# First norm of a hybrid encoder layer: squares, scaling and turns beside the modulation products, scale and shift by channel block

## The chip, the cores and the metric

The kernel runs on one core of a Trainium2 chip. The metric is the device time of one execution in microseconds (us). The engines are TensorE (PE, its weight loads PEld), VectorE (DVE), ScalarE (ACT), GpSimd (POOL) and SyncE (SP); each runs its own list of instructions in order, and they meet at semaphores. SP, ACT and POOL also issue transfers.

## The reference, cut to what matters

One step of an encoder layer over 1024 prompt rows and 8 x 16 sample rows, D = 1024, all float32. The part around the change:

```python
mod = (jax.nn.silu(c) @ w_ada[l] + b_ada[l])[:, None, :]
sh_m, sc_m, g_m, sh_f, sc_f, g_f = jnp.split(mod, 6, axis=-1)
h = rmsnorm(x, norm_mix_w[l]) * (1.0 + sc_m) + sh_m
...
z, xbc, dt, q, k, v = jnp.split(h @ w_in, SPLITS, axis=-1)
xbc, new_conv = causal_dwconv(xbc, conv_hist, conv_w, conv_b)
```

`c` has nine rows (one for the prompt, one for each sample). After this follow a scan over chunks, attention, an output projection, and a second norm with a gated feed-forward network.

## The kernel before

**Numbers in two parts.** The large products are computed as three products of numbers rounded to fp32r: every operand is split into a high part (a rounding copy) and a low part (the operand less its high part). A weight unit is 128 columns of a weight matrix (128x1024 elements). SP loads it into one of three buffers of `weights_raw`, ACT makes `weights_hi` (`w_hi(n)`), POOL makes `weights_lo` (`w_lo(n)`), and PE multiplies. SP loads unit n when the low part of unit n-3 is made; `w_hi(n)` waits for the products of unit n-3.

**Setup and modulation ("ada" phase, 0 to 44 us).** SP issues 20 small loads (`setup_in`), then four pieces of `w_ada` of 2 MB into three buffers `WA`. PE waits for all 20, turns the rows of `c` (after a SiLU on ACT) and the small vectors, and multiplies the turned condition `cond_T` with the pieces: per piece eight products of 128x32 by 128x512, a copy of the result into `mod_rows` on DVE (semaphore `ada_row`), and a sum over partition groups on PE (`ada_sum`), to which DVE adds the bias (`ada_out`). Pieces 0, 1 give the shift `SCOL[:, 0]`, pieces 2, 3 the scale `AM`, both as columns by channel. All engines meet at `phase_end`.

**First norm (44 to 106 us).** `norm_tiles` goes over nine tiles of 128 rows. ACT issues the load of a tile into one of two buffers `x_rows`, takes the squares with their sum (L1726) and the root (L1727); DVE takes the reciprocal (L1126) and scales the rows (L1127); PE turns the tile by eight transposes of 128x128 (L514) into two banks; DVE applies scale and shift from the banks, one instruction for each channel block of 128 (L1104; for the sample tile two, L1116 and L1117) into `h_raw`; ACT copies it to `h_hi` (L1720) and POOL makes `h_lo` (L2132). Both have shape [128, 8 channel blocks, 1152 rows].

**Input projection (from 106 us).** `in_unit(n)` multiplies unit n with three groups of 384 rows, 24 instructions to a group (L571 to L573), into banks 0 to 2 in turn. Units 0 to 7 are the channels of the convolution: ACT copies each group from its bank (`proj_out`, L1770 and L1774), DVE convolves a unit (L1175 to L1181) once its three groups are out, and ACT applies a SiLU (`xbc_silu`). Groups 0 and 1 of unit 0 stand between the turns of the first norm, and so do four of the `late_pair`s: a late pair multiplies two more pieces of 0.5 MB of `w_ada` (32 pieces in all, for the other four sections of the modulation), and `late_sum` sums a section. The rest of them stand in `late_slot(n)`, behind unit n. SP's queue holds, in order, the four pieces, units 0 to 2, pairs 0 and 1, and so on; a pair's pieces wait for the products of an earlier pair.

The order on PE after the phase's end:

```python
for j in range(NT):
    turn_tile(0, j, HNORM, BANKS_1)
    if j in (5, 8):
        in_unit(0, [j // 3 - 1])
    if j in PAIRS_AT_NORM:
        late_pair(PAIRS_AT_NORM.index(j))
in_unit(0, [2])
late_slot(0)
for n in range(1, 9):
    in_unit(n)
    if n < 7:
        late_slot(n)
```

Of the kernel before, what the change touches and what calls it, by code (L numbers as in the profile page):

```python
# [78 lines left out]
def build(nc, a, o):  # L79
# [93 lines left out]
    HL = r("h_lo", [P, KT, T], F32R)  # L173
    XBC = at("xbc_T", [P, 8, T], R2)
    ZT = at("z_T", [P, 4, T], R3)
    r = Region(R2 + 4 * T * 4, R3)
    HNORM = r("x_normed", [P, 2, D])
    HRAW = r("h_raw", [P, 2, KT, P])
# [11 lines left out]
    CT = r("cond_T", [P, KT, 32])  # L190
    TAILR = at("ssm_tail_rows", [27, D], xr_off)
# [114 lines left out]
    with ctx:  # L306
# [17 lines left out]
        def mark(ins, name):  # L324
# [6 lines left out]
            "pe_once": ["dt_raw", "dt_turned", "tails_turned", "sums", "state_turned", "yo_rows", "bias_turned", "ffn_turned"],  # L331
# [46 lines left out]

        def unit_used(n):

            if n < N_OUT0:
                return sem("proj"), 3 * (n + 1)
# [54 lines left out]
        N_SETUP = 20  # L437
        OUT_NORM_AT = [4, 6]
        BANKS_1, BANKS_2 = [4, 6] * 5, [6, 6, 6, 4, 6, 4]
# [13 lines left out]
        PAIRS_AT_NORM = [2, 4, 6, 8]  # L453
# [3 lines left out]
        def _(sp):  # L457
# [22 lines left out]
            for c in range(4):  # L480
                if c >= 3:
                    sp.wait_ge(sem("ada_used"), c - 2)
                sp.dma_start(WA[c % 3][:, :, :], a["w_ada"][0, :, c * 512:(c + 1) * 512]
                             .rearrange("(k p) n -> p k n", p=P)).then_inc(sem(f"ada_in{c % 3}"), 16)
# [25 lines left out]
        def _(pe):  # L510
# [5 lines left out]
            pe.wait_ge(sem("setup_in"), 16 * N_SETUP)  # L516
            pe.wait_ge(*once("cond_silu"))
            for k in range(KT):
                turn(PS[:, 0, k * NCOND:(k + 1) * NCOND], CROWS[:, k * P:(k + 1) * P], NCOND)
            turn(PS[:, 0, 80:101], VROW[:, :], 21)  # L520
            turn(PS[:, 0, 104:152], BROW[:, :], 48).then_inc(sem("setup_turned"), 1)
            for k in range(KT):
                mm = turn(PS[:, 1, k * 29:(k + 1) * 29], SROW[:, k * P:(k + 1) * P], 29)
            mm.then_inc(sem("setup_turned"), 1)
            pe.matmul(PS[0:NH, 2, 0:384], RELB[:, :], ONEHOT[:, :], start=True, stop=True)\
              .then_inc(sem("setup_turned"), 1)

# [11 lines left out]
            pe.wait_ge(*once("cond_T"))  # L539
            for c in range(4):  # L540
# [8 lines left out]
                if c >= 1:  # L549
# [39 lines left out]
            def late_sum(s):  # L589
                pe.wait_ge(sem("ada_row"), 4 + s + 1)  # L590
                if s == 0:
                    pe.wait_ge(sem("h_raw"), 2 * NT)
                else:
                    pe.wait_ge(sem("ada_sum_out"), 4 + s)
# [16 lines left out]
            def in_unit(n, groups=range(NG)):  # L611
                weights_ready(pe, n)
                for g in groups:
                    if n == 0:
                        pe.wait_ge(sem("h_lo"), 3 * (g + 1))
                    q = 3 * n + g
                    if q >= 3:
                        pe.wait_ge(sem("proj_out"), q - 2)
                    mm = products(PS[:, q % 3, 0:TG],
                                  [(WH[n % 3][:, k * P:(k + 1) * P], WL[n % 3][:, k * P:(k + 1) * P],  # L620
                                    HH[:, k, g * TG:(g + 1) * TG], HL[:, k, g * TG:(g + 1) * TG]) for k in range(KT)])
                    mm.then_inc(sem("proj"), 1)


            for j in range(NT):
                turn_tile(0, j, HNORM, BANKS_1)
                if j in (5, 8):
                    in_unit(0, [j // 3 - 1])
                if j in PAIRS_AT_NORM:
                    late_pair(PAIRS_AT_NORM.index(j))  # L630
            in_unit(0, [2])
            late_slot(0)
            for n in range(1, 9):
                in_unit(n)
                if n < 7:
                    late_slot(n)
# [295 lines left out]
            for g in range(3):  # L932
                for f in range(KT):
# [27 lines left out]
                    if g == 2 and f in OUT_NORM_AT:  # L961
                        turn_tile(NT, OUT_NORM_AT.index(f), N2, BANKS_2)

            turn_tile(NT, 2, N2, BANKS_2)
            pe.wait_ge(sem("mix_out"), 18)
            for j in range(3, 5):
                turn_tile(NT, j, N2, BANKS_2)
# [8 lines left out]
            for i, (u, g) in enumerate(UP_ORDER):  # L976
                weights_ready(pe, N_FFN0 + u)
                if i in (0, 3):
                    pe.wait_ge(sem("h_lo"), NT + 3 * (g + 1))
# [3 lines left out]
                if i < 1:  # L983
                    turn_tile(NT, 6 - 1 + i, N2, BANKS_2)

            def turn_late(jj):
                pe.wait_ge(sem("normed"), NT + 6 + jj + 1)
                if jj == 0:
                    pe.wait_ge(sem("up_out"), NUP0)
                else:  # L990
                    pe.wait_ge(sem("h_raw"), 2 * (NT + 6 + jj))
# [6 lines left out]
            for s, (kind, grp, i) in enumerate(MIXED):  # L998
                n = N_MIXED + s
                weights_ready(pe, n)  # L1000
                if kind == "u":
                    if i == 0:
                        pe.wait_ge(sem("h_lo"), NT + NT)
# [39 lines left out]
        def _(ve):  # L1043
# [7 lines left out]

            ve.wait_ge(sem("setup_in"), 16 * N_SETUP)
            ch(ve.tensor_tensor(LQK[:, 0, :], LQK[:, 0, :], LQK[:, 1, :], ALU.mult))
            ch(ve.tensor_tensor(LQK[:, 2, :], LQK[:, 2, :], LQK[:, 3, :], ALU.mult))
# [1251 lines left out]
```

## Time and profile before

| | |
|---|---|
| median of 3 runs | 1859.39 us (1858.83 to 1861.01) |
| the profiled execution | 1859.56 us, its span 1857.8 us |
| mean granted TensorE clock | 0.946 of full speed |
| PE busy | 1651.0 us (89%) |
| DVE busy | 986.8 us (53%) |
| ACT busy | 628.7 us (34%) |
| POOL busy | 443.2 us (24%) |
| read from HBM, written | 173.62 MB, 17.11 MB |

The span is counted from the first to the last instruction. An engine's busy time counts its instructions alone; in a row of the profile the time in square brackets is the idle time just before it, with what ended it. "Granted clock" is the share of full speed (2.4 GHz) that TensorE was given. Where PE is busy throughout, its work sets the time; where it is not, the question is which engine or transfer it waits for.

### The profile page before, as it was taken

How to read it: one execution, taken by the hardware profiler on the slowest of the kernel's cores; microseconds unless marked ns; L12 is line 12 of the kernel's file. 1: busy time of each engine (PE TensorE's matmuls, PEld its weight loads, DVE VectorE, ACT ScalarE, POOL GpSimd, SP SyncE). 2: the span in 40 equal slices, each digit the busy share in tenths (PEclk: the TensorE clock that was granted, in tenths of full speed). 3: DMA queues.
4: the chain of work that ended last, by engine and by line, in shares of the span. 5: the costliest groups of instructions: out<-in, count | busy, mean ns of one | idle time of the engine just before them, and what ended most of it. 6: DMA issues, size and time to landing. Idle time of an engine off the chain costs nothing. (4 is left out here: it accounts for less than half of the span.)

```text
span 1857.8 us, 23796 instructions
## 1 busy us (share of the span) xinstructions
PE 1651.0 (89%) x9399; PEld 1461.4 (79%) x9399; DVE 986.8 (53%) x1686; ACT 628.7 (34%) x1137; POOL 443.2 (24%) x270
## 2 busy tenths in 40 slices
PE   4489998779998987758968999999999999999896
PEld 1378987659996665637758999999978988999775
DVE  1665515860003665453345666666546677667744
ACT  1422222302112663342242222322444444444532
POOL 0331111113220000026554333323261111111132
PEclk9689999979998998978988999999999999999998
DMA  8545110112123002605561222122245434444442
GB/s 284 191 151 170 35 35 3 45 45 67 48 83 131 1 1 69 227 12 146 192 227 45 64 64 68 57 68 81 68 128 167 132 107 147 134 150 125 145 155 72
DMA packets 164564, 192.27 MB, mean 103 GB/s; under 512 B 7858, under 2 KB 126875, under 8 KB 164416
## 3 DMA queue, kind: packets, MB, share of 16 engines
q1 hardware_dynamic: 139626, 132.11, 23.1%
q10 hardware_dynamic: 19612, 40.93, 6.8%
q0 software_dynamic: 5216, 17.71, 2.7%
q8 instruction: 75, 1.23, 0.3%
q14 instruction: 35, 0.29, 0.0%
HBM read 173.62 MB, written 17.11 MB: 103 GB/s over the span
## 5 line engine op out<-in xcount | busy, mean ns | idle before, releaser
L571 PE MATMUL PS<-h_hi,weights_hi 128*128 128x384 f32 x1280 | 436.6, 341 | 11.0 <-POOL h_lo L2132 6.4
L572 PE MATMUL PS<-h_lo,weights_hi 128*128 128x384 f32 x1280 | 433.9, 339 | 0.0
L573 PE MATMUL PS<-h_hi,weights_lo 128*128 128x384 f32 x1280 | 433.6, 339 | 0.0
L2119 POOL TENSOR_TENSOR weights_lo<-weights_raw,weights_hi 128x1024 fp32r<-128x1024 f32 x99 | 252.7, 2554 | 754.2 <-ACT weights_hi L1697 731.9
L1697 ACT ACTIVATE weights_hi<-weights_raw 128x1024 fp32r<-128x1024 f32 x202 | 213.7, 1058 | 217.8 <-PE PS L1022 105.0
L571 PEld LDWEIGHTS PS<-h_hi,weights_hi 128*128 128x128 f32 x1280 | 244.1, 191 | 17.9 <-issue 13.2
L572 PEld LDWEIGHTS PS<-h_lo,weights_hi 128*128 128x128 f32 x1280 | 244.0, 191 | 0.0
L573 PEld LDWEIGHTS PS<-h_hi,weights_lo 128*128 128x128 f32 x1280 | 243.7, 190 | 0.0
L1020 PE MATMUL PS<-weights_hi,g_hi 128*128 128x512 f32 x396 | 160.9, 406 | 15.2 <-DVE weights_lo L1644 12.9
L2247 POOL TENSOR_TENSOR g_lo<-g_T,g_hi 128x384 fp32r<-128x384 f32 x66 | 81.6, 1237 | 372.3 <-ACT g_hi L2014 372.3
L1021 PE MATMUL PS<-weights_lo,g_hi 128*128 128x512 f32 x396 | 158.9, 401 | 0.0
L1022 PE MATMUL PS<-weights_hi,g_lo 128*128 128x512 f32 x396 | 158.3, 400 | 0.0
L1644 DVE TENSOR_TENSOR weights_lo<-weights_raw,weights_hi 128x1024 fp32r<-128x1024 f32 x103 | 124.3, 1235 | 25.5 <-ACT weights_hi L1697 22.9
L572 PE MATMUL PS<-h_lo_b,weights_hi 128*128 128x384 f32 x352 | 118.5, 337 | 0.0
L571 PE MATMUL PS<-h_hi_b,weights_hi 128*128 128x384 f32 x352 | 118.4, 336 | 0.0
L573 PE MATMUL PS<-h_hi_b,weights_lo 128*128 128x384 f32 x352 | 118.4, 336 | 0.0
L1020 PEld LDWEIGHTS PS<-weights_hi,g_hi 128*128 128x128 f32 x396 | 75.6, 191 | 34.2 <-DVE weights_lo L1644 15.0
L1022 PEld LDWEIGHTS PS<-weights_hi,g_lo 128*128 128x128 f32 x396 | 75.7, 191 | 18.2
L1021 PEld LDWEIGHTS PS<-weights_lo,g_hi 128*128 128x128 f32 x396 | 76.1, 192 | 15.6
L1554 DVE SCALAR_TENSOR_TENSOR val<-up_val,ffn_conv_cols,val 128x768 f32<-128x768 f32 x44 | 83.7, 1903 | 1.6
L1554 DVE SCALAR_TENSOR_TENSOR gate<-up_gate,ffn_conv_cols,gate 128x768 f32<-128x768 f32 x44 | 83.3, 1894 | 1.5
L2032 ACT ACTIVATE up_val<-PS 128x384 f32<-128x384 f32 x44 | 21.6, 491 | 141.4 <-PE PS L573 141.4
(365 smaller groups left out, 2526.8 us busy)
## 6 DMA issues: line engine op xcount, KB each, us to landing
weights_raw<-in_w_up_dram SPq DMA_DIRECT2D x88, 512.0 KB, 3.9
weights_raw<-in_w_down_dram SPq DMA_DIRECT2D x66, 512.0 KB, 4.5
w_ada_unit<-in_w_ada_dram SPq DMA_DIRECT2D x32, 512.0 KB, 5.6
weights_raw<-in_w_in_dram SPq DMA_DIRECT2D x24, 512.0 KB, 4.1
weights_raw<-in_w_out_dram SPq DMA_DIRECT2D x24, 512.0 KB, 4.1
w_ada<-in_w_ada_dram SPq DMA_DIRECT2D x4, 2048.0 KB, 16.1
k_cache<-in_cache_k_dram ACTq DMA_DIRECT2D x8, 1024.0 KB, 5.6
x_scratch<-x_new POOLq DMA_DIRECT2D x9, 512.0 KB, 6.2
```

What stands on the lines that cost most here:

```text
L571: pe.matmul(out, wh, xh, start=(i == 0), stop=False)
L572: pe.matmul(out, wh, xl, start=False, stop=False)
L573: mm = pe.matmul(out, wl, xh, start=False, stop=(i == n - 1))
L1020: pe.matmul(out, GH[i % 2][:, lhs], WH[n % 3][:, ws], start=(f == 0), stop=False)
L1021: pe.matmul(out, GH[i % 2][:, lhs], WL[n % 3][:, ws], start=False, stop=False)
L1022: mm = pe.matmul(out, GL[i % 2][:, lhs], WH[n % 3][:, ws], start=False, stop=(f == FT - 1))
L1554: ins = ve.scalar_tensor_tensor(out=d, in0=src, scalar=w, in1=d, op0=ALU.mult, op1=ALU.add)
L1644: mark(ve.tensor_tensor(WL[n % 3][:, :], WR[:, n % 3, :], WH[n % 3][:, :].bitcast(F32), ALU.subtract), "w_lo_dve")
L1697: mark(ac.activation(WH[n % 3][:, :], WR[:, n % 3, :], ACT.Copy), "w_hi")
L2032: mark(ac.activation(U[:, 2 + g * TG:2 + (g + 1) * TG], PS[:, i % 8, 0:TG], ACT.Copy), "up_out")
L2119: mark(gp.tensor_tensor(WL[n % 3][:, :], WR[:, n % 3, :], WH[n % 3][:, :].bitcast(F32), ALU.subtract), "w_lo")
L2247: mark(gp.tensor_tensor(GL[i % 2][:, :], GT[:, f, gg * TG:(gg + 1) * TG], GH[i % 2][:, :].bitcast(F32), ALU.subtract), "g_lo")
```

## The change

- The nine tiles of x are loaded at the very start from ACT's queue into a buffer of their own, `XIN` (it lies where `xbc_T` lies later). SP's queue begins with the two loads of `c`, the constants (together a semaphore `cond_in`) and pieces 0 and 1 of `w_ada`; then come the other 17 small loads (`setup_in`), then pieces 2 and 3.
- In the ada phase, the tiles go in three groups of three. ACT takes squares and roots; DVE scales three tiles in place (`x_norm`); PE turns them (`x_turn`), four channel blocks to bank 2 and four to bank 3; DVE copies the first half back into `XIN` (`x_out`), ACT the second. A group stands ahead of each of the products with pieces 0, 1 and 2. The turns of the small vectors and their copies stand behind the products with piece 0.
- `w_lo(0)` and `w_lo(1)` on POOL stand ahead of the end of the phase.
- After the phase, for each group of 384 rows and each channel block, ACT writes `h_hi` from `XIN` with scale and shift in one instruction (128x384, `mod_hi`), and DVE makes `h_lo` in two: x times scale less `h_hi`, then plus shift (`mod_lo`). In the last group the blocks have 256 prompt rows, and the sample rows go by themselves in four wide instructions. POOL makes no `h_lo` here.
- PE does late pairs 0 and 1, then group 0 of units 0 and 1, pair 2, group 1 of both, pair 3, group 2 of both, and then each late slot ahead of a unit from unit 2 on. ACT copies the groups out in that order, and the SiLU of unit 0's convolution stands directly behind the sixth copy.
- `norm_tiles` of the second norm counts its semaphores from 0; nothing else there changes.

```diff
+XIN = at("x_T", [P, NT, KT, P], R2)
-HNORM = r("x_normed", [P, 2, D])
-HRAW = r("h_raw", [P, 2, KT, P])
+XSQ = at("x_squares_unread", [P, 3, D], R4)
...
 # SP
-setup(CONST[:, :], const_dram[:, :])
-setup(CROW[0:1, :], a["c_prompt"])
-setup(CROW[1:NCOND, :], a["c_sample"])
+sp.dma_start(CROW[0:1, :], a["c_prompt"]).then_inc(sem("cond_in"), 16)
+sp.dma_start(CROW[1:NCOND, :], a["c_sample"]).then_inc(sem("cond_in"), 16)
+sp.dma_start(CONST[:, :], const_dram[:, :]).then_inc(sem("cond_in"), 16)
+ada_in(0)
+ada_in(1)
 setup(VROW[0:8, :], ...)
...
-for c in range(4):
-    if c >= 3:
-        sp.wait_ge(sem("ada_used"), c - 2)
-    sp.dma_start(WA[c % 3][:, :, :], ...)
+ada_in(2)
+ada_in(3)
...
 # PE
+def x_turn(j):
+    pe.wait_ge(sem("x_normed"), j + 1)
+    for half in range(2):
+        if j >= 1:
+            pe.wait_ge(sem("xT_act" if half else "xT_dve"), j)
+        for k in range(4 * half, 4 * half + 4):
+            mm = turn(PS[:, 2 + half, k % 4 * P:(k % 4 + 1) * P], XIN[:, j, k, :])
+        mm.then_inc(sem("x_turned"), 1)
...
 for c in range(4):
+    if c < 3:
+        for j in range(3 * c, 3 * c + 3):
+            x_turn(j)
+    ada_products(c)
+    if c == 0:
+        setup_turns()
+    else:
+        ada_sum(c - 1)
 ada_sum(3)
...
+late_pair(0)
+late_pair(1)
+for g in range(NG):
+    in_group(0, g)
+    in_group(1, g)
+    if g < 2:
+        late_pair(2 + g)
+for n in range(2, 9):
+    late_slot(n - 2)
     in_unit(n)
...
 # DVE
 for c in range(4):
+    if c < 3:
+        x_norm(c)
+        for j in range(3 * c, 3 * c + 3):
+            x_out(j)
     ve.wait_ge(sem("ada_used"), c + 1)
...
+def modulate(g):
...
+    for k in range(KT):
+        x = XIN[:, 3 * g:3 * g + n, k, :]
+        ve.wait_ge(sem("mod_hi"), KT * g + k + 1)
+        ch(ve.scalar_tensor_tensor(out=x, in0=x, scalar=AM[:, k, 0:1],
+                                   in1=HH[:, k, cols].bitcast(F32).rearrange("p (j n) -> p j n", j=n),
+                                   op0=ALU.mult, op1=ALU.subtract))
+        mark(ve.tensor_scalar(HL[:, k, cols].rearrange("p (j n) -> p j n", j=n), x,
+                              SCOL[:, 0, k, 0:1], None, ALU.add), "mod_lo")
...
 # ACT
+for j in range(NT):
+    load(XIN[:, j, :, :], x_all[j].rearrange("p (k n) -> p k n", k=KT), f"x_in{j // 3}")
+ac.wait_ge(sem("cond_in"), 48)
 out(ac.activation(CROWS[:, :], CROW[:, :], ACT.Silu), "act_once")
+for g in range(3):
+    ac.wait_ge(sem(f"x_in{g}"), 48)
+    for j in range(3 * g, 3 * g + 3):
+        mark(ac.activation(XSQ[:, j % 3, :]..., XIN[:, j, :, :], ACT.Square, accum_out=STAT[:, 48 + j:49 + j]), "act_step")
+    again(ac, "act_step")
+    mark(ac.activation(STAT[:, 3 * g:3 * g + 3], STAT[:, 48 + 3 * g:51 + 3 * g], ACT.Sqrt, ...), "x_sd")
+    for j in range(3 * g, 3 * g + 3):
+        ac.wait_ge(sem("x_turned"), 2 * j + 2)
+        mark(ac.activation(XIN[:, j, 4:8, :], PS[:, 3, :]..., ACT.Copy), "xT_act")
 w_hi(0)
 w_hi(1)
...
+        mark(ac.activation(HH[:, k, cols]..., XIN[:, 3 * g:3 * g + n, k, :],
+                           ACT.Identity, scale=AM[:, k, 0:1], bias=SCOL[:, 0, k, 0:1]), "mod_hi")
```

## Rows read from the trace of the kernel before

**Rows 1.** The page's chain that ended last, shares by engine.

```profile
PE 40%; DVE 4%; POOL 1%; ACT 1%; issue 1%; DMA 0%; DVEq 0%; ACTq 0%
```

**Rows 2.** Windows: stretch, length, busy us (count) of PE, PEld, DVE, ACT, POOL, clock, DMA, GB/s.

```profile
14.00:38.00 24.00, 15.23 (x84) 6.08 (x84) 5.27 (x16) 0.97 (x1) 0.66 (x1) 1.00 1.05 387
...
44.20:106.50 62.30, 30.16 (x152) 22.32 (x152) 38.65 (x99) 25.57 (x40) 26.03 (x12) 0.67 0.52 174
106.50:128.60 22.10, 22.01 (x116) 18.93 (x116) 10.96 (x17) 2.48 (x5) 5.19 (x3) 0.92 0.45 145
128.60:263.00 134.40, 134.40 (x811) 118.64 (x811) 64.26 (x99) 35.62 (x57) 22.67 (x10) 1.00 0.30 97
```

**Rows 3.** Timeline of the ada phase: start us, length us, engine, instruction.

```profile
8.75 15.43 SPq L483 DMA_DIRECT2D w_ada<-in_w_ada_dram  x4
...
13.92 1.05 ACT L1700 ACTIVATE cond_silu<-cond_rows 9x1024 f32<-9x1024 f32 x1 [11.90 <-DMA lambda_vectors<-in_lambda_k_dram]
...
18.97 0.18 DVE L1058 COPY vector_cols<-PS 128x21 f32<-128x21 f32 x1 [4.05 <-PE PS L525]
...
27.19 3.64 PE L546 MATMUL PS<-w_ada,cond_T 128*32 128x512 f32 x16 [3.44 <-DMA w_ada<-in_w_ada_dram]
...
32.60 1.93 PE L546 MATMUL PS<-w_ada,cond_T 128*32 128x512 f32 x16 [0.47 <-DMA w_ada<-in_w_ada_dram]
...
34.45 1.06 PE L535 MATMUL PS<-CONST,mod_rows 128*128 128x9 f32 x8
34.64 0.69 DVE L1078 COPY mod_rows<-PS 128x512 f32<-128x512 f32 x1 [2.21 <-PE PS L546]
...
43.85 0.23 DVE L1084 SCALAR_TENSOR_TENSOR scale_mix_cols<-mod_cols,vector_cols 128x72 f32<-128x72 f32 x1
```

**Rows 4.** The line of the four loads of `w_ada` pieces, L483: issue to landing.

```profile
DMA to landing us min/median/max: 10.4/16.1/22.7
```

**Rows 5.** Waits from 44.2 to 106.5 us: total us, times, longest.

```profile
ACT x_normed L1726 <- DMA x_rows<-in_x_prompt_dram: 20.0, 6, 5.3
```

**Rows 6.** Timeline of the first norm, one tile's instructions and a later turn.

```profile
58.75 1.06 ACT L1726 ACTIVATE x_normed<-x_rows 128x1024 f32<-128x1024 f32 x1 [2.07 <-DMA x_rows<-in_x_prompt_dram]
...
60.82 0.75 DVE L1127 TENSOR_SCALAR x_normed<-x_rows,stats 128x1024 f32<-128x1024 f32 x1 [0.30 <-DVE stats L1126]
...
61.63 1.97 PE L514 MATMUL PS<-CONST,x_normed 128*128 128x128 f32 x8 [1.44 <-DVE x_normed L1127]
...
73.81 1.09 PE L514 MATMUL PS<-CONST,x_normed 128*128 128x128 f32 x8 [1.33 <-DVE x_normed L1127]
```

**Rows 7.** Timeline of PE where it becomes busy throughout.

```profile
106.59 0.66 PE L571 MATMUL PS<-h_hi,weights_hi 128*128 128x384 f32 x1 [5.74 <-POOL h_lo L2132]
...
112.47 1.46 PE L597 MATMUL PS<-mod_rows_late,CONST 128*9 128x512 f32 x3
...
116.00 0.45 PE L571 MATMUL PS<-h_hi,weights_hi 128*128 128x384 f32 x1
...
128.69 1.92 PE L584 MATMUL PS<-w_ada_unit,cond_T 128*32 128x512 f32 x16
```

**Rows 8.** Timeline of DVE, POOL and ACT in the first convolution.

```profile
113.24 0.75 DVE L1175 TENSOR_SCALAR conv_acc<-conv_in,ssm_conv_cols 128x1024 f32<-128x1024 f32 x1 [3.95 <-ACT conv_in L1774]
113.91 0.28 DVE L1176 TENSOR_SCALAR conv_acc<-conv_in,ssm_conv_cols 128x128 f32<-128x128 f32 x1
...
114.15 2.37 POOL L2119 TENSOR_TENSOR weights_lo<-weights_raw,weights_hi 128x1024 fp32r<-128x1024 f32 x1 [5.39 <-ACT weights_hi L1697]
114.22 3.38 DVE L1178 SCALAR_TENSOR_TENSOR conv_acc<-conv_in,ssm_conv_cols,conv_acc 128x1024 f32<-128x1024 f32 x1
...
117.90 1.28 DVE L1178 SCALAR_TENSOR_TENSOR conv_acc<-conv_in,ssm_conv_cols,conv_acc 128x1024 f32<-128x1024 f32 x1
119.10 0.35 DVE L1181 SCALAR_TENSOR_TENSOR conv_acc<-conv_in,ssm_conv_cols,conv_acc 128x128 f32<-128x128 f32 x1
...
120.48 0.49 ACT L1770 ACTIVATE conv_in<-PS 128x384 f32<-128x384 f32 x1 [6.40 <-PE PS L573]
```

More of the change, by code:

```diff
@@ L537, in ada_sum, with ada_products @@
                 mm.then_inc(sem("ada_summed"), 1)
-            pe.wait_ge(*once("cond_T"))
-            for c in range(4):
+            def ada_products(c):
                 pe.wait_ge(sem(f"ada_in{c % 3}"), 16 * (c // 3 + 1))
@@ L548, in _ @@
                 mm.then_inc(sem("ada_used"), 1)
-                if c >= 1:
+            pe.wait_ge(*once("cond_T"))
+            for c in range(4):
+                if c < 3:
[5 more added lines that the diff above has]
+                else:
                     ada_sum(c - 1)
@@ L1059, in _, with x_norm @@
[L1059 removed]
             ch(ve.memset(CT[:, :, :], 0.0))
+            ve.wait_ge(*once("cond_turned"))
             out(ve.tensor_copy(CT[:, :, 0:NCOND], PS[:, 0, 0:72].rearrange("p (k c) -> p k c", k=KT)), "dve_once")
[L1062 to L1064 removed]
+            def x_norm(g):
+                ve.wait_ge(sem("x_sd"), g + 1)
+                ch(ve.reciprocal(STAT[:, 16 + 3 * g:19 + 3 * g], STAT[:, 3 * g:3 * g + 3]))
+                for j in range(3 * g, 3 * g + 3):
+                    mark(ve.tensor_scalar(XIN[:, j, :, :], XIN[:, j, :, :], STAT[:, 16 + j:17 + j], None, ALU.mult), "x_normed")
@@ L1080, in _ @@
                     ada_out(c - 1)
+                else:
+                    setup_cols()
             ada_out(3)
@@ L1751, in _, with in_rows_out, xbc_silu @@
             load(WDT[:, :, :], a["w_in"][0, :, 1536:1544].rearrange("(k p) n -> p k n", p=P), "wdt_in")
-            for n in range(12):
+            def in_rows_out(n, g):
+                q = IN_ORDER.index((n, g))
+                ac.wait_ge(sem("proj"), q + 1)
+                src = PS[:, q % 3, 0:TG]
+                if n >= 8:
+                    mark(ac.activation(ZT[:, n - 8, g * TG:(g + 1) * TG], src, ACT.Silu), "proj_out")
+                    return
+                R = XRAW[:, n % 2, :]
+                c1 = min(TG, SEQ - g * TG)
+                ins = ac.activation(R[:, 3 + g * TG:3 + g * TG + c1], src[:, 0:c1], ACT.Copy)
+                if c1 < TG:
+                    mark(ins, "act_step")
+                    smp = R[:, 3 + SEQ:XB_W].rearrange("p (b t) -> p b t", b=NB)
+                    ins = ac.activation(smp[:, :, 3:3 + TS], src[:, c1:TG].rearrange("p (b t) -> p b t", b=NB), ACT.Copy)
+                mark(ins, "proj_out")
+            def xbc_silu(c):
+                ac.wait_ge(sem("conv"), c + 1)
+                mark(ac.activation(XBC[:, c, :], CACC[:, c % 2, :], ACT.Silu, bias=SSMC[:, c, 4:5]), "xbc_silu")
+            w_hi(2)
+            for q in range(6):
+                in_rows_out(*IN_ORDER[q])
+                if q == 4:
+                    w_hi(3)
+            xbc_silu(0)
+            for n in range(2, 12):
                 w_hi(n + 2)
@@ L2126, in _ @@
             gp.wait_ge(sem("bias_out"), 16)
+            w_lo(0)
+            w_lo(1)
             phase_end(gp, "ada")
@@ L2133, in norm_tile @@
                                       hi[:, :, c0:c0 + P].bitcast(F32), ALU.subtract), "h_lo")
-            w_lo(0)
-            w_lo(1)
-            for jj in range(NT):
-                norm_tile(0, jj, HRAW, HH, HL)
             for n in range(12):
```

201 lines of the change are left out of this document (103 added, 98 removed).

## The prediction, made before the changed kernel was run

> **What bounds the kernel now.** I read four views, in this order. The chain that ended last puts PE first by a wide margin [rows 1], so PE's idle stretches are where time can be won. The windows show where those are: from 106.5 us PE is busy 22.0 of 22.1 us and then 134.4 of 134.4 us, while from 44.2 to 106.5 us it is busy 30.2 of 62.3 us at a granted clock of 0.67 [rows 2]. The reader is to see there that in this stretch no engine is near full (DVE, the busiest, 38.7 of 62.3 us) and that the transfers are half used: it is a chain of single tiles. Third, the waits name its longest link: ACT waits six times, 20.0 us in all, for a tile of x, because two buffers let a load begin only when an earlier tile is done [rows 5]. Fourth, the timeline of the ada phase: the engines stand still until all 20 small loads are in (13.92 us), and from 14 to 38 us the transfers move 387 GB/s without a gap, PE waiting for each piece of `w_ada` [rows 2, 3]. So the ada phase is bound by transfers and the norm by a round trip, and the one could run beside the other.
>
> The measure of the change is when PE reaches unit 2 with nothing behind it. Before, unit 1 ends at 128.5 us, just before the pairs of late slot 1 (128.69) [rows 7]. In both orders the same work follows from there (late slot 1 and unit 2 only change places), and PE never waits up to 263 us [rows 2], so what is saved at this point stays saved unless something new stops PE later.
>
> **The change: transfers at the start.** Large transfers began to flow near 12 us (the first landed at 19.15, less its own 5.4 and a little of x, both worked out below); now almost nothing small stands before them, and I take 3 us. Data up to the last piece: 8.4 MB of `w_ada`, 4.7 MB of x, 0.64 MB of constants and 0.2 MB of small rows, 14 MB; at 0.387 MB/us [rows 2] 36 us, so the last piece lands near 40 us, against 38 before. How do the two queues share? Piece 0 was issued at 8.75 and landed 10.4 us later, at 19.15, with products on piece 1 from 27.19 and on piece 2 from 32.60 [rows 3, 4]. Piece 2 took 5.4 us alone, piece 1 8.0 us with two tiles of x (1.05 MB) beside it; the two tiles cost about 2.7 us of the common rate. I take half and half, 0.195 MB/us each. Then: constants near 6.3 us, the first three tiles near 11, piece 0 near 17, all of x near 27, piece 1 near 27.5, and the 17 small loads, which stand behind piece 1 in SP's queue, near 30 us. Bounds: 27 if they overtake, 33 if they are slow as at the start. Piece 3 is issued after the first products (about 26 us) while the queue is still full, and costs nothing.
>
> **The ada phase as a chain.** Squares of three tiles, root and reciprocal: 2.07 us for the last (58.75 to 60.82) and 2 x 1.2 before it, 4.5 us, and 0.75 for the scaling [rows 6]. First group from 11 us: PE can turn at about 17.5 (with 1.3 us allowed for ACT's first use of the root), three tiles by 1.97 us, 6 us, then products 3.64 us: near 26. The next link is the small loads, which hold PE's `setup_turns` and with them DVE's `setup_cols`, behind which `x_norm(1)` is queued. From 30.0:
>
> - the turns of the small vectors, about 3.1 us (from the SiLU's end at 14.97 to 18.97 PE turned condition and small vectors [rows 3]; I give the condition 0.9), and five copies of 1.8 us: 34.9;
> - reciprocal and one scaling: 35.9;
> - three tiles of turns: 1.97 us each at a low clock, 1.09 at the high one [rows 6], where the copy of half a bank (0.69 [rows 3]) keeps the period above 1.35. 4.0 to 5.9 us, taken 5.1: 41.0;
> - ACT can begin the third group's squares only behind its copies of the second: 0.6 + 3.9 + 0.3, 45.8. Products with piece 1 (1.93 to 3.64) and their sum (1.06 [rows 3]) run beside it;
> - reciprocal, scaling, turns, 0.95 + 4.8: 51.5;
> - products 2, sum, products 3, two sums with a copy of 0.69 between: 2.5 + 0.9 + 2.5 + 0.9 + 0.9: 59.2;
> - bias, `scale_cols` 0.23 [rows 3], meeting: 60.0.
>
> Products 1.93 at one end, 3.64 at the other, and the turns likewise, give 56 and 66 us for this point; it was 44.1 us. So the ada phase grows by 16 us. Which of PE's two levels holds is the largest unknown: the same 16 instructions took 3.64 us at 27.19 and 1.93 at 32.60, after PE had worked on [rows 3]; 1.93 is 2.4 GHz. I take values between, nearer the high level towards the end, since there PE has few gaps.
>
> **From there to the first product.** ACT writes a block of `h_hi` in about 0.5 us (0.49 for 128x384 out of a bank [rows 8]), DVE is slower and sets the pace. The scalar_tensor_tensor took 1.28 us at 1024 columns and 0.35 at 128, so 1.04 ns a column and 0.22 fixed: 0.62 at 384. The tensor_scalar took 0.75 at 1024 and 0.28 at 128 [rows 8], so 0.42 at 384, 0.34 to the next start. With the wait between, 0.98 us a block, 7.9 for eight; 9.4 if writing fp32r halves the second's rate, 7.0 if starts overlap more. First product at 60.0 + 0.6 + 7.9 = 68.5 us. Pairs 0 and 1 are on PE before it; their 2.1 MB, asked for at about 57, take 5.4 us and 2 of start, near 64.5, and are covered, by a microsecond or two at most.
>
> **From the first product on.** Three groups of unit 1 took from 116.00 to 128.5, 4.16 us each; the start at a low clock costs 1.65 more, as before (106.59 to 112.4 for the first [rows 7]). Six groups 24.9, low start 1.65, pairs 2 and 3 at 0.96 each, late slot 0 of 3.6 us (112.4 to 116.0 [rows 7]): unit 2 starts 32.1 us after the first product, at 100.6. Against 128.5 that is 27.9 us gained.
>
> Does DVE keep up? Group 1 is ready 7.9 us after group 0, and PE needs it after 10.9. Group 2 has eight blocks of 256 (0.79 us each) and three DVE instructions of 1.2 to 1.3 us on the sample rows: 10.1 us more, 18.0, against 20.2. Cover is 2.2 us. POOL's `w_lo(2)`, however, falls into group 2. In the convolution a DVE instruction that began beside `weights_lo` took 3.38 us where its like took 1.28 [rows 8]; 2.1 us, just covered. ACT's copies: the first group's copy stands behind all 25 instructions of `mod_hi`, three DMA issues and `w_hi(2)`, about 20.5 us after the meeting, and PE's fourth group needs it at about 21: nothing. `xbc_silu(0)` now stands directly behind the sixth copy and waits for a convolution of 8 to 10 us; queued behind it are `w_hi(4)` and unit 2's copies. It is ready about 37 us after the first product; PE fills its next three banks from 32 to 44.5, so that nothing waits. POOL loses nine `h_lo` of 2.4 us and DVE 64 small instructions: no gain, since neither was the bound.
>
> The Trainium skill, "SBUF — State Buffer", section "Who interferes with whom", says that a DVE instruction with two SBUF inputs, or one in a two-port mode, and a GpSimd instruction that reads SBUF exclude each other for the whole instruction. The trace agrees (3.38 against 1.28 us [rows 8]). By this rule the low parts of a group, once moved to DVE, are exposed to `w_lo(2)`, and `w_lo(0)`, `w_lo(1)` to DVE's scalings in the ada phase; it would add at most two of POOL's instructions, 4.7 us, an estimate that leaves the sign as it is.
>
> **Sum.** The profiled execution took 1859.56 us, 0.2 from the median of 1859.39, so the difference is taken from the median: 1859.4 - 27.9 = 1831.5 us. Own range of this case: the meeting at 56 to 66, blocks 7.0 to 9.4 for the group, a stall in group 2 of 0 to 4: gain 17 to 33, 1826 to 1842.
>
> **Rivals.**
> - *The slow ada phase.* PE stays at 1.2 GHz through all of it and the small loads land at 33 us: the meeting at 69, first product 77.5, gain 19, 1840 us. For: 0.67 in the norm stretch, where PE also worked in pieces [rows 2]. Against: PE has more work per gap now. The Trainium skill, "TensorE: Matmul & The Clock Gate", section "HAM oscillation — how this bites in real kernels", describes such a fall-back when work waits for data.
> - *DVE becomes the bound.* Blocks at 1.2 us and collisions with POOL in both later groups: first product 1.6 us later, stalls of about 6: gain 20, 1839 us. For: [rows 8]. Against: POOL has one instruction in the stretch.
> - *A quicker chain.* x and the small loads land early, turns at 1.09: meeting at 54, gain 34, 1825 us.
> - *Nothing gained.* PE is not held by the norm, and the later stages wait for a load or DVE at the same absolute time. Against: every later load waits for earlier products, and PE has no waits to 263 us. 1859 us.
> - *Slower.* The convolution becomes the bound of units 2 to 8. It starts with one unit more behind it, and each POOL instruction holds DVE for 2.1 us. DVE is busy 64 of 134 us there [rows 2]; a unit with its late slot takes PE 14.5 us. It decides from 18.5 us of DVE chain a unit, over seven units 28 us; at 19.5 it would be 35 - 27.9, 1866 us. The rows leave over 5 us of slack per unit.
>
> **Chances.** Forecast 0.55, slow ada phase 0.17, DVE the bound 0.10, quicker chain 0.11, nothing gained 0.03, slower 0.04. About 0.2% (3.7 us) is what a measurement of this kernel tells from no change. Faster 0.93, within 0.03, slower 0.04. The range 1822 to 1845 leaves out the last two, the far end of the quicker chain and mixtures of the two slow ones.
>
> **What the changed profile would show.** The small loads in near 30 us, with PE and DVE idle before; DVE's `scale_cols` at 56 to 66 us; blocks of `mod_lo` at about 1 us; the first L571-like product at 64 to 73 us; no PE wait over 1 us after it up to unit 2, which starts near 100; and later stages shifted by the same amount as that. Wrong would be: x taking more than its half of the rate and piece 0 late, blocks over 1.3 us, or PE waiting for `mod_lo` of groups 1 and 2.

## The result, and the profile after

The changed kernel took 1844.2 us (median of six executions, 1837.16 to 1850.38) against 1859.45 (1858.28 to 1863.74) of the kernel before: a ratio of 0.9914, 95% interval 0.9891 to 0.9937. It is faster, by 0.9%. The time lies in the range given last in the prediction (1822 to 1845), 0.8 us below its upper end, and above the range that it had added up from its own terms (1826 to 1842): 15.3 us were gained where 27.9 were forecast and 17 was the least. The profiled execution took 1844.83 us, its span is 1843.0 us, its mean granted clock 0.945 (0.946 before).

The chain that ended last is PE's still, by the page, and PE is busy for 90% of the span:

```profile
PE 41%; DVE 4%; POOL 1%; ACT 1%; issue 1%; DMA 0%; DVEq 0%; ACTq 0%
```

The windows of the changed kernel (columns as in [rows 2]):

```profile
14.00:38.00 24.00, 9.62 (x52) 5.88 (x52) 5.85 (x12) 5.77 (x12) 0.00 (x0) 0.77 0.94 331
0.00:14.00 14.00, 0.99 (x8) 0.92 (x8) 0.51 (x2) 6.57 (x9) 0.20 (x4) 1.00 0.88 329
...
106.00:244.00 138.00, 138.00 (x831) 119.39 (x829) 70.49 (x110) 35.70 (x57) 23.79 (x11) 1.00 0.35 114
43.90:65.00 21.10, 17.48 (x118) 11.44 (x116) 8.55 (x17) 8.28 (x14) 4.68 (x2) 0.84 0.26 68
```

From 14 to 38 us the transfers move 331 GB/s where they moved 387, and PE, which had 15.2 of 24 us of work there [rows 2], has 9.6. From 43.9 to 65 us it is busy 83% of the time. From 106 to 244 us it never stops, as in the same stretch of work before.

The timeline has the dates that the prediction names: first of PE and DVE in the ada phase, then of DVE and POOL in the modulation, then of PE again.

```profile
22.14 1.92 PE L568 MATMUL PS<-w_ada,cond_T 128*32 128x512 f32 x16 [1.10 <-DMA w_ada<-in_w_ada_dram]
...
35.50 0.29 PE L527 MATMUL PS<-CONST,vector_rows 21*128 21x21 f32 x1 [11.44 <-DMA lambda_vectors<-in_lambda_k_dram]
...
41.19 5.92 PE L527 MATMUL PS<-CONST,x_T 128*128 128x128 f32 x24 [2.79 <-DVE x_T L1088]
...
57.89 1.92 PE L568 MATMUL PS<-w_ada,cond_T 128*32 128x512 f32 x16
```

```profile
64.92 0.23 DVE L1131 SCALAR_TENSOR_TENSOR scale_mix_cols<-mod_cols,vector_cols 128x72 f32<-128x72 f32 x1
66.07 0.62 DVE L1210 SCALAR_TENSOR_TENSOR x_T<-x_T,scale_mix_cols,h_hi 128x384 f32<-128x384 f32 x1 [0.91 <-ACT h_hi L1830]
66.72 0.61 DVE L1213 TENSOR_SCALAR h_lo<-x_T,mod_cols 128x384 fp32r<-128x384 f32 x1
67.25 0.61 DVE L1210 SCALAR_TENSOR_TENSOR x_T<-x_T,scale_mix_cols,h_hi 128x384 f32<-128x384 f32 x1
...
89.45 0.35 DVE L1213 TENSOR_SCALAR h_lo<-x_T,mod_cols 128x256 fp32r<-128x256 f32 x1
...
90.23 2.38 DVE L1213 TENSOR_SCALAR h_lo<-x_T,mod_cols 128x256 fp32r<-128x256 f32 x1
```

```profile
89.98 2.48 POOL L2217 TENSOR_TENSOR weights_lo<-weights_raw,weights_hi 128x1024 fp32r<-128x1024 f32 x1 [25.61 <-ACT weights_hi L1766]
```

```profile
75.69 0.66 PE L602 MATMUL PS<-h_hi,weights_hi 128*128 128x384 f32 x1 [2.25 <-DVE h_lo L1213]
...
76.15 0.52 PE L603 MATMUL PS<-h_lo,weights_hi 128*128 128x384 f32 x1
...
81.54 0.34 PE L602 MATMUL PS<-h_hi,weights_hi 128*128 128x384 f32 x1
...
109.40 0.45 PE L602 MATMUL PS<-h_hi,weights_hi 128*128 128x384 f32 x1
```

The reader is to see four dates. All small loads are in at 35.5 us (forecast 30.0). `scale_cols`, DVE's row at 64.92 (`scale_mix_cols`), starts there (60.0 for it and the meeting behind it), 29.4 us later, where the chain was worked out at 30.0. The first product follows 10.77 us after it (8.5), at 75.69 (68.5). Unit 2 starts 33.7 us after that (32.1), at 109.40 (100.6). The whole of 8.8 us at unit 2 is in these rows: 5.5 - 0.6, 2.3 and 1.6.

In what follows, "the lead" is how much earlier than in the kernel before PE has the same number of instructions left. It is read where the kernel before stands at 290 us, and at the end. The changed kernel leads by 19.1 us at 290, by 18.2 at 700, by 14.2 at 960 and by 14.7 at the end. So 4.4 us more went in later stages, nearly all around the attention.

### The profile page after: what moved, and what is told of

It reads as the page before. It is cut to its first block and busy times, and to the rows that moved or that the text cites. A ratio compares the mean times of both kernels' runs of the same rounds, so it can differ in the third digit from the quotient of the medians.

```text
span 1843.0 us, 23788 instructions
## 1 busy us (share of the span) xinstructions
PE 1652.8 (90%) x9399; PEld 1464.0 (79%) x9399; DVE 990.8 (54%) x1660; ACT 636.7 (35%) x1156; POOL 424.3 (23%) x261
## 5 line engine op out<-in xcount | busy, mean ns | idle before, releaser
L602 PEld LDWEIGHTS PS<-h_hi,weights_hi 128*128 128x128 f32 x1280 | 243.7, 190 | 16.9 <-issue 12.2
L1048 PEld LDWEIGHTS PS<-weights_hi,g_hi 128*128 128x128 f32 x396 | 75.8, 191 | 34.2 <-DVE weights_lo L1713 14.7
```

The source lines that it names most:

```text
L602: pe.matmul(out, wh, xh, start=(i == 0), stop=False)
L1048: pe.matmul(out, GH[i % 2][:, lhs], WH[n % 3][:, ws], start=(f == 0), stop=False)
```

## Why the small loads come so late

SP's timeline shows an order that the forecast had not: the first of the 17 small loads blocks its queue for 13.31 us behind the two pieces, so that the others are issued from 18.27 to 25.06 us.

```profile
1.86 3.01 SPq L475 DMA_DIRECT2D w_ada<-in_w_ada_dram  x2
4.92 13.31 SPq L466 DMA_DIRECT2D vector_rows<-in_norm_mix_w_dram  x1
18.27 0.59 SPq L466 DMA_DIRECT2D vector_rows<-in_norm_ffn_w_dram  x1
...
25.11 7.00 SPq L475 DMA_DIRECT2D w_ada<-in_w_ada_dram  x2
```

The queues' packets in two stretches show how they shared and what the small loads are. From 13 to 19 us (q10 is ACT's queue with x, q1 SP's with `w_ada`):

```profile
DMA packets 845, 2.40 MB, mean 400 GB/s; under 512 B 48, under 2 KB 48, under 8 KB 845
...
q10 hardware_dynamic: 423, 1.54, 65.4%
q1 hardware_dynamic: 422, 0.86, 37.8%
```

and from 24 to 36 us:

```profile
DMA packets 2679, 3.22 MB, mean 268 GB/s; under 512 B 1148, under 2 KB 1249, under 8 KB 2679
```

The queues took turns by packets, 423 to 422. A packet of x holds 3.6 KB and one of `w_ada` 2.0 KB, so that x got 64% of the bytes, not half. Piece 0 came at 22.1 instead of 17. The Trainium skill, "DMA: Bandwidth & Descriptors", section "Queues, rings and completion order", says that each DMA engine goes round its queues packet by packet; the trace agrees (423 and 422). That x takes more than half and piece 0 comes late is the first of the prediction's own signs of being wrong. And 1148 packets of under 512 B, the small loads, pass in 12 us in which the transfers move 268 GB/s. The kernel before has them too, in its first 14 us, where its engines stand still:

```profile
DMA packets 1653, 1.51 MB, mean 108 GB/s; under 512 B 1151, under 2 KB 1252, under 8 KB 1653
```

The small loads are in 10.4 us after SP has issued the last of them (25.06). Whether the block at SP, the place behind piece 1, or these packets cost the 5.5 us was for the experiments to say.

## The experiments

Each ratio is to the kernel before in the same batch, with its 95% interval. The profiled marks are "`scale_cols` / first product / unit 2"; for the changed kernel they are 64.92 / 75.69 / 109.40.

### The small loads ahead of the pieces

```diff
+setup(VROW[0:8, :], ...)      # all 17
-ada_in(0)
-ada_in(1)
-setup(VROW[0:8, :], ...)      # all 17
+ada_in(0)
+ada_in(1)
```

> The 17 small loads stand ahead of the pieces of w_ada in SP's queue. Theory (SP's queue was blocked: the first small load took 13.3 us to issue behind the two big pieces, so the small loads landed at 35.5 us and held PE and DVE): they land near 13 us, scale_cols ends near 53 us instead of 65, the first product of unit 0 comes at about 63 instead of 75.7, and the time falls by 10 to 13 us against the changed kernel, to about 1832. Rival (the transfers set the ada phase: 14 MB at 0.387 MB/us): the pieces come later instead, PE waits for pieces 2 and 3, scale_cols stays above 61 us and the time falls by less than 4 us.

1841.6 us, ratio 0.9876 (0.9837 to 0.9914); 61.57 / 72.34 / 105.66. The wait for the small loads is gone, but piece 0 is now what PE waits for:

```profile
28.78 3.40 PE L568 MATMUL PS<-w_ada,cond_T 128*32 128x512 f32 x16 [6.75 <-DMA w_ada<-in_w_ada_dram]
```

The queues from 8 to 18 us:

```profile
DMA packets 1607, 3.28 MB, mean 328 GB/s; under 512 B 750, under 2 KB 837, under 8 KB 1607
...
q10 hardware_dynamic: 826, 3.01, 87.8%
q1 hardware_dynamic: 781, 0.27, 12.1%
```

In turn with x, SP's queue spent its 781 packets on 0.27 MB. My theory, 10 us or more from this order, fell. The rival came out in its numbers (`scale_cols` above 61 us, less than 4 us of time) and in its kind: a piece comes late instead. It is piece 0 that PE waits for, not pieces 2 and 3. The mark moved by 3.4 us.

### The small loads from POOL's queue

```diff
 # POOL, first in its list
+def gp_setup(dst, src):
+    store(dst, src, "setup_in")
+gp_setup(VROW[0:8, :], ...)   # all 17, taken out of SP's queue
```

> The 17 small loads are issued by POOL, SP issues the pieces of w_ada back to back. Theory (blocked queue): the small loads land by about 20 us, nothing stops SP between pieces 1 and 2, and the gain is that of the kernel with the small loads first or 1 us more, to about 1831. Rival (transfers set the phase): less than 4 us of gain. Second rival (POOL's issues are slow beside DVE): small loads at 30 us or later and half of the gain.

1842.3 us, ratio 0.9893 (0.9857 to 0.9929); 60.93 / 71.69 / 105.01. The theory (about 1831) fell, and the first rival (less than 4 us of gain) came out. SP issues the pieces from 1.86 us on with no small load among them, and PE waits for piece 0 until 28.43:

```profile
28.43 3.24 PE L552 MATMUL PS<-w_ada,cond_T 128*32 128x512 f32 x16 [6.82 <-DMA w_ada<-in_w_ada_dram]
```

The queues from 8 to 18 us, q0 being POOL's with the small loads:

```profile
q10 hardware_dynamic: 409, 1.47, 42.0%
q0 software_dynamic: 410, 0.28, 34.6%
q1 hardware_dynamic: 410, 0.84, 26.7%
```

Three queues take turns here, 409 to 410 to 410 packets, and SP's gets a third of them. So moving the small loads away from the block at SP is not enough: what they and x take from the transfers then lands on piece 0.

### The small loads between pieces 0 and 1

```diff
 ada_in(0)
-ada_in(1)
 setup(VROW[0:8, :], ...)      # all 17
+ada_in(1)
 ada_in(2)
```

> The 17 small loads stand behind piece 0 and ahead of piece 1 in SP's queue. Theory (two causes share the ada phase: with the small loads behind two pieces SP's queue was blocked to 18.3 us; with them ahead of all pieces piece 0 came at 28.8 us, because the loads of x take about two thirds of the transfers while they last): piece 0 lands near 22 us, the small loads near 24, nothing else waits for a transfer, scale_cols ends at 54 to 57 us against 64.9 of the changed kernel and 61.6 with the small loads first, and unit 2 starts 8 to 10 us earlier than in the changed kernel; the time is 1833 to 1838. Rival (the chain of turns and copies sets the phase whatever the loads do): scale_cols at 61 us or later, 1841.

1836.94 us, ratio 0.9885 (0.9863 to 0.9907); 59.61 / 70.38 / 103.69.

```profile
22.75 3.55 PE L568 MATMUL PS<-w_ada,cond_T 128*32 128x512 f32 x16 [1.59 <-DMA w_ada<-in_w_ada_dram]
...
29.48 0.23 PE L527 MATMUL PS<-CONST,vector_rows 21*128 21x21 f32 x1 [3.18 <-DMA lambda_vectors<-in_lambda_k_dram]
```

and its packets from 20 to 28 us:

```profile
DMA packets 1754, 1.56 MB, mean 195 GB/s; under 512 B 1049, under 2 KB 1150, under 8 KB 1754
```

Piece 0 keeps its date within 0.6 us. SP has issued the last small load at 19.27 us, 5.8 earlier, they are in 6.0 us earlier (10.2 after that issue) and `scale_cols` comes 5.3 us earlier: with the small loads where the forecast had put them (29.5 against 30.0), the mark falls where it had put it (59.6 against 60.0). The time (1833 to 1838) was hit, but `scale_cols` at 54 to 57 and unit 2 8 to 10 us earlier (it is 5.7) were too bright by what the small loads need, 29.5 instead of 24: 1049 small packets pass in the 8 us from 20 to 28, with the rate down to 195 GB/s. At 0.387 MB/us [rows 2] the 1.56 MB would have taken 4.0 us of these 8, and the 3.22 MB from 24 to 36 us in the changed kernel 8.3 of 12: by this estimate the small loads cost the transfers about 4 us in both places, and the stretches in which they pass are 8 and 12 us long. The run moves the small loads out from behind the block and ahead of piece 1 at once, so it doesn't tell these two apart; it does show that their date is what the mark follows.

### DVE's second instruction on one row of 384

In the changed kernel the second instruction reads x as three pieces of 128 (one per tile). Here the first writes to a contiguous scratch, and the second reads 384 columns.

```diff
-ch(ve.scalar_tensor_tensor(out=x, in0=x, ...))
-mark(ve.tensor_scalar(HL[:, k, cols].rearrange("p (j n) -> p j n", j=n), x, ...), "mod_lo")
+m = MTMP[:, k % 2, 0:n * P]
+ch(ve.scalar_tensor_tensor(out=m.rearrange("p (j n) -> p j n", j=n), in0=x, ...))
+mark(ve.tensor_scalar(HL[:, k, cols], m, ...), "mod_lo")
```

> DVE's first instruction of a block writes to a contiguous scratch row of 384, the second reads it from there, so that both sides of the second have one dimension of 384. Theory (the second took 0.61 us at 384 columns but 0.35 at 256 because its operands' outer dimensions, 3 and 384, keep it from the double rate, not because it writes fp32r): it takes 0.42 us, a block 0.98 instead of 1.17, the first product comes 1.5 us earlier, 1842 to 1843. Rival (384 columns into fp32r are slow in any shape): 0.61 us again and no change.

1844.25 us, ratio 0.9902 (0.9874 to 0.993); 64.58 / 73.82 / 106.62.

```profile
65.71 0.62 DVE L1212 SCALAR_TENSOR_TENSOR mod_tmp<-x_T,scale_mix_cols,h_hi 128x384 f32<-128x384 f32 x1 [0.90 <-ACT h_hi L1832]
66.36 0.42 DVE L1215 TENSOR_SCALAR h_lo<-mod_tmp,mod_cols 128x384 fp32r<-128x384 f32 x1
```

0.42 us instead of 0.61, for the same columns, written as fp32r in both: it is the shape of the operand, not fp32r writing, to which the prediction had put its bound of 9.4 us. The rows of the changed kernel say the same: 128x256, two pieces of 128, takes 0.35. The Trainium skill, "VectorE: DVE Perf Modes", section "What auto-detection actually checks", gives the double rate to a source and a destination whose outermost dimensions are both even, or equal. The trace agrees for two pieces (0.35) and for one row of 384 (0.42); three pieces against three, if the destination counts as such, would be equal and miss it all the same (0.61), which no run here goes into. The first product comes 9.24 us after `scale_cols` instead of 10.77. Unit 2 starts 32.8 us after the first product (33.7 in the changed kernel's first profile, 33.3 in its second). The lead at 290 us is 21.9, up from 19.1 (20.8 in a second execution of the changed kernel, below); the time of the whole (1842 to 1843 expected) doesn't show it, for a reason that the section on the spread comes to.

### Units 0 and 1 one after the other

```diff
 for g in range(NG):
     in_group(0, g)
-    in_group(1, g)
     if g < 2:
         late_pair(2 + g)
+in_unit(1)
```

> Units 0 and 1 no longer alternate: PE does the three groups of unit 0, then those of unit 1. Theory (DVE makes a group in 9.4 us, PE needs 4.2 for one unit): PE waits about 4 us for group 1 and again for group 2, unit 2 starts 7 to 8 us later, about 1852. Rival (the alternation is worth nothing, DVE is ahead anyway): 1844.

1852.48 us, ratio 0.9949 (0.9932 to 0.9966); 63.76 / 74.53 / 117.71. PE now waits for DVE, by the waits from 62 to 125 us (total, times, longest):

```profile
PE PS L602 <- DVE h_lo L1217: 6.5, 1, 6.5
...
PE PS L602 <- DVE h_lo L1213: 5.1, 2, 3.0
```

where the changed kernel has a single wait of this kind, before its first product:

```profile
PE PS L602 <- DVE h_lo L1213: 2.2, 1, 2.2
```

The theory came out, with waits of 3.0 and 6.5 us behind the first product where 4 and 4 were expected. The alternation is worth about 8 us of the gain (unit 2 is 9.5 us later relative to the first product). In the changed kernel's profile it just covers DVE's instruction of 2.38 us beside POOL's `weights_lo`; without it nothing covers that instruction.

### PE kept at work ahead of the first product

```diff
+for i in range(26):
+    turn(PS[:, 7, 0:P], C("ident"))
 late_pair(0)
 late_pair(1)
+for i in range(12):
+    turn(PS[:, 7, 0:P], C("ident"))
```

> PE does 26 idle turns of the identity into an unread bank ahead of pair 0 and 12 behind pair 1, otherwise the changed kernel. Theory (the first products run at 1.2 GHz to 81.3 us because PE was mostly idle from 64.7 to 75.7, and this costs 2.8 us): the clock is at 2.4 GHz from the first product on, the group takes 4.2 us instead of about 7, unit 2 starts 2 to 3 us earlier relative to the first product. The time falls by 2 us or less than the spread shows. Rival (the turns delay the pairs and the first product): first product later than 76.5, no gain or a loss of 1 us.

1846.77 us, ratio 0.9933 (0.991 to 0.9955); 66.08 / 76.84 / 110.15. The first products run at 0.34 us each from the start, 2.4 GHz, and group 0 of unit 0 takes 4.24 us instead of 6.88. But unit 2 still comes 33.3 us after the first product. What the products no longer take, PE now waits for. These are PE's waits on the way (the first is the one for group 0's low parts, as in every version):

```profile
76.84 0.41 PE L602 MATMUL PS<-h_hi,weights_hi 128*128 128x384 f32 x1 [1.01 <-DVE h_lo L1217]
...
91.45 0.42 PE L602 MATMUL PS<-h_hi,weights_hi 128*128 128x384 f32 x1 [0.68 <-ACT conv_in L1851]
...
98.12 0.41 PE L602 MATMUL PS<-h_hi,weights_hi 128*128 128x384 f32 x1 [1.27 <-issue]
```

The row at 98.12 is the start of group 2, 21.28 us after the first product. It names no releaser, but DVE's last low part of that group ends just before:

```profile
96.80 1.22 DVE L1221 TENSOR_TENSOR h_lo<-x_T,h_hi 128x1024 fp32r<-128x1024 f32 x1
```

Group 2 starts 21.28 or 21.29 us after the first product in four profiles without idle turns too (the changed kernel once more, and the small loads in each of their three other places), and unit 2 33.3 us after it in all five. Only the first profile of the changed kernel, whose group 0 was the slowest of these (6.88 us, against 5.80 to 6.38), has 21.65 and 33.7. So with these blocks DVE sets the date of group 2, and the expected 2 to 3 us weren't there. The rival's mark (first product later than 76.5, no gain) was met, but not by its cause: the first product follows `scale_cols` by 10.76 us as everywhere, and `scale_cols` itself, ahead of the idle turns, was 1.2 us late.

### All three, and without the idle turns

> The small loads behind piece 0, the contiguous scratch for DVE's second instruction, and the idle turns of PE, all three. Theory (the shortfall up to unit 2 is the sum of the three): scale_cols at 54 to 57 us, first product 9.2 us later at 64 to 66, unit 2 at 96 to 99 us against 109.4 of the changed kernel and 100.6 forecast; a time of 1829 to 1834. Rival (what is won at unit 2 is given back in the attention stage, whatever the clock does): lead of 30 us over the kernel before at unit 2, less than 18 at the end, 1841 or more in all runs.

The small loads between the pieces, the row of 384 and the idle turns: 1833.93 us, ratio 0.9867 (0.9849 to 0.9885); 58.82 / 68.06 / 99.86, lead 27.1 at 290 us, 25.8 at the end. The time was as expected (1829 to 1834) and the rival fell (25.8, not less than 18), but `scale_cols` and unit 2 were again 1 to 2 us later than expected. The forecast's own marks (60.0 / 68.5 / 100.6, 27.9) come out once its three wrong terms are put right.

> The small loads behind piece 0 and the contiguous scratch, without the idle turns of PE. Theory (from the run with the idle turns: with the clock already high PE only waits for DVE's low parts of group 2, so the turns bring nothing that lasts): unit 2 at 99 to 102 us as with the turns (100.3), time within 2 us of its 1833.9. Rival (the turns were worth their 2.8 us): unit 2 at 103, time 1836 to 1838.

Without the idle turns: 1838.95 us, ratio 0.9861 (0.9835 to 0.9888); 58.98 / 68.22 / 101.07, lead 27.4 at 290 us, 20.7 at the end. Unit 2 is where the theory had it (99 to 102), but the time is 5.0 us above that of the run with the turns, not within 2. The ratios, each to its own batch, hardly differ (0.9867 and 0.9861). From the first product to unit 2 it is 31.8 us with the turns and 32.85 without (32.8 with the row of 384 alone), so the turns are worth about 1.0 us when DVE is quick enough, from single profiles, and nothing that a ratio can tell.

### The third group's squares ahead of the second's copies

On top of the last version; ACT's order only.

```diff
+x_squares(0)
+x_copies(0)
+x_squares(1)
+x_squares(2)
+x_copies(1)
+x_copies(2)
```

> As the kernel with the small loads behind piece 0 and the scratch, and ACT takes the third group's squares ahead of its copies of the second group's turns, where it is idle. Theory (the squares of group 3 behind the copies end 0.9 us after DVE could scale, 51.28 against 50.37 us in the changed kernel): scale_cols comes 0.7 to 1.2 us earlier than without, unit 2 too, a time of 1832 to 1835. Rival (the scaling waits for the products with piece 1 and their sum as long): less than 0.4 us.

1835.5 us, ratio 0.9846 (0.9812 to 0.9881), the best ratio of all, though its interval overlaps that of the last version; 59.17 / 68.41 / 101.92. The reciprocal of the third group stands 1.1 us earlier, at 44.23:

```profile
44.23 0.18 DVE L1087 RECIPROCAL stats<-stats 128x3 f32<-128x3 f32 x1
```

but the products with piece 2, three rows of PE's timeline later, took part of their time at the low clock and gave it back:

```profile
51.09 2.97 PE L569 MATMUL PS<-w_ada,cond_T 128*32 128x512 f32 x16
```

(1.92 in the version without the edit). The expected 0.7 to 1.2 us at `scale_cols` was missed, and the time by 0.5 us; whether it is there at an equal clock stays open.

### The changed kernel once more: the spread

> The changed kernel once more, unchanged. Theory (the differences of several us between its own executions, and between its lead of 19 us at unit 2 and 14.7 at the end, are the granted clock's): its executions spread over 8 us or more again, the longer ones at a lower mean clock, about 1.9 us for each thousandth of the mean clock; the low stretches between 560 and 960 us are others than in the first profile, and so is the lead lost there. Rival (the lead is lost to a wait that the changed kernel has in the attention stage): the same 3 to 4 us lost in the same place, and PE idle for longer there.

1842.11 us, ratio 0.9906 (0.9886 to 0.9927); 63.61 / 74.37 / 107.68. The marks of one program thus differ by 1.3 to 1.7 us between two profiles. Three more versions are the same program up to `scale_cols` (64.58, 63.76 and 66.08), so that this mark spreads over 2.5 us in five profiles. By that measure the small loads first (61.57) or on POOL (60.93) are worth at least 2.0 us there, and between the pieces (58.8 to 59.6 in four profiles) at least 4.0. The distance from `scale_cols` to the first product is 10.76 or 10.77 us in every profile with the old blocks and 9.24 in every one with the row of 384. Its lead is 20.8 us at 290 and 20.7 at the end: nothing was lost in the attention. The windows of equal work there (in the kernel before, the first changed execution, and this one):

```profile
740.00:930.00 190.00, 151.08 (x1073) 116.95 (x1066) 78.23 (x156) 61.30 (x116) 66.31 (x39) 0.88 0.46 145
```

```profile
721.90:915.40 193.50, 154.55 (x1073) 119.13 (x1062) 78.23 (x156) 61.40 (x116) 66.39 (x39) 0.87 0.44 142
```

```profile
719.10:909.50 190.40, 149.13 (x1073) 115.40 (x1067) 78.27 (x156) 61.42 (x116) 66.39 (x39) 0.88 0.45 144
```

The same 1073 matmuls, DVE, ACT and POOL busy for the same time within 0.1 us; PE's busy time differs, 154.6 against 149.1 us, while its idle time goes the other way, 39.0 against 41.3. The first changed execution lost 3.5 us there and this one 0.4, with the same program. The other profiles sort the same way: between 290 us and the end, the seven with a mean granted clock of 0.940 to 0.947 gave back 3.4 to 9.8 us of their lead, three of the four with 0.949 to 0.951 gave back 0.1 to 1.3 us and the fourth gained 2.3. Over the twelve executions of the changed kernel the times go from 1837.16 to 1850.38 us and their mean granted clocks from 0.943 to 0.952, with a correlation of -0.95: about 1.5 us for a thousandth of clock (1.9 was expected). That the clock is the cause rests on this correlation and on PE's busy time at equal work; no run sets the clock.

## Why the prediction was right, and by how much it missed

- **What bounds, and that the norm can run beside the ada phase.** Right. PE reaches unit 2 at 109.4 instead of 128.5 us, with no stop behind it up to 244 us.
- **Transfers, "I take half and half, 0.195 MB/us each".** Wrong: the queues shared by packets, x got 64% of the bytes and piece 0 came at 22.1 instead of 17. PE lost nothing by that date in the changed kernel, where it stood idle for 11.4 us after these products, until the small loads were in. Whether the smaller share also kept SP's queue blocked for longer, and so the small loads late, no run separates.
- **"The 17 small loads ... near 30 us", bounds 27 to 33.** This is the term that failed most, 5.5 us: 35.5. It lies outside its own bounds. It counted their bytes (0.2 MB; the profile's list of issues adds up to 0.34) and not their 1148 packets, and it had no block at SP. With the small loads in at 29.5 us, in the run between pieces 0 and 1, the mark was 59.6. The kernel before had shown both the packets (1151 up to 14 us) and what they take (13.92 us, [rows 3]), and the prediction used that only for its upper bound of 33.
- **The chain from there, 30.0 us.** 29.4 to the start of `scale_cols`. The parts lie within about a microsecond of the forecast and partly cancel: from the small loads to the turns 5.7 (5.9 forecast), three tiles of turns 5.92 (5.1 taken, 4.0 to 5.9 given), up to the third group's reciprocal 4.2 (4.8); the products with pieces 1 to 3 took 2.04, 1.92 and 1.92.
- **"0.98 us a block".** 1.18: the second instruction took 0.61 where the rate of a contiguous row was used; 0.42 with one. The bound of 9.4 us for eight blocks was hit; its reason, fp32r, was not the right one. That is 1.5 us over eight blocks; with 0.5 more from `scale_cols` to DVE's first block (1.15 us, 0.6 forecast) and 0.2 up to PE's start, 2.3 us.
- **"1.65 for the start at a low clock".** The first 18 products came at 0.32 us intervals; the two groups took 11.1 us, 2.8 more than 2 x 4.16. The groups after them took 8.53 a pair, 0.2 more than forecast. 1.6 us in all for this profile. But the clock's own share of that is 0.4: with the start at the high clock unit 2 still comes 33.3 us after the first product, 1.2 more than forecast, because of the next term.
- **"DVE keeps up", cover 2.2 us, `w_lo(2)` costs 2.1.** Wrong by a microsecond. The low parts of group 2 were forecast 18.0 us after the first product, 20.1 with the collision, and PE at 20.2; they come at 21.2 in every profile with the old blocks. Group 1 took 9.4 us (7.9), which is the error of the blocks a second time, and group 2 took 11.9 with the collision (12.2). The collision itself was sized right: 2.38 us instead of 0.35, so 2.0. The Trainium skill's rule on the shared port that the prediction cites ("SBUF — State Buffer", section "Who interferes with whom") held here for an instruction with one source, and of POOL's instructions only `w_lo(2)` cost DVE anything. Taking the alternation away made the stall plain (11.6 us of waits against 2.2). With the row of 384 the low parts come at 19.7.
- **"What is saved at this point stays saved".** It holds for work and waits: no later wait took the place of the old one. In a single execution it doesn't hold for what the clock takes: the profiled one gave 4.4 us back, the second one 0.1.
- **The sum.** 27.9 - 4.9 - 2.3 - 1.6 - 4.4 = 14.7 us, the lead at the end. The median says 15.3. The forecast had no term for the last of these. That the time still fell inside the range given is in part luck: the range ended at 1845, two of the six executions lay above it (1845.58 and 1850.38), and the small loads (27 to 33) and the first product (64 to 73) lay outside their bounds. The lead of 19.1 at unit 2 is that of the rival "slow ada phase" (19), and by the size of the gain that rival lay closer than the forecast. Its cause was not this one: from 43.9 to 65 us the clock was 0.84, not PE at 1.2 GHz throughout. The late small loads alone make up most of what it had put together from both. "DVE the bound" had its blocks of 1.2 us right and the size of its stalls wrong: about 6 us forecast, and behind the first product none in the first profile and 0.1 to 0.7 in four others with the same blocks and without idle turns.

## What to carry to other kernels

Cost a load by its packets as well as by its bytes: here a thousand packets of under 512 B passed in stretches of 8 and 12 us, and beside another queue each of them spent a turn that a 2 KB packet would have had (781 packets for 0.27 MB). When a step is moved ahead of the point where a new chain begins, date that point first: here 6.0 us at the small loads were 5.3 at `scale_cols` and 5.7 at unit 2, more than any other error of this forecast. When one engine is to stay just ahead of another, an error in its instruction can count twice: here 1.5 us at the first product and about 1 more at group 2. And when a change of 0.5% is measured on an engine-bound kernel, compare marks inside the profiles at equal work, since the whole spread by 0.7% over executions of one program.

## What the runs showed that was not expected

- An issue on SP behind two loads of 2 MB blocked the queue for 13.31 us, though its own load has 4 KB; behind one such load the 17 issues took 0.3 to 3.4 us each.
- Two queues got 423 and 422 packets in 6 us; their bytes were 1.54 and 0.86 MB. Three queues got 409, 410 and 410 in 10 us.
- tensor_scalar of 128x384: 0.61 us as three pieces of 128, 0.42 as one row; two pieces, 128x256, 0.35.
- Twelve executions of one program spread by 13.2 us, and the time followed the mean granted clock.
- The low clock at the start of a stretch cost nothing at unit 2 where DVE set the date of group 2 (33.3 us from the first product with the idle turns, and in four profiles without), 0.4 us in the one profile whose start was slowest, and about 1.0 us when DVE was quicker (32.8 against 31.8).
